# Hybrid mixer and mixture-of-experts layer: head outputs laid tile by tile, an earlier first weight load, and a new order in the expert steps

## What is computed

```python
def hybrid_mixer(h, w_in, ...):
    ...
    o = jnp.concatenate([o_a, o_b], axis=-1).astype(h.dtype)
    return o @ w_out

def hierarchical_moe(h, w_rg, b_rg, w_re, b_re, w_gate, w_up, w_down):
    g_probs = jax.nn.softmax((hf @ w_rg + b_rg).astype(jnp.float32), axis=-1)
    g_p, g_idx = lax.top_k(g_probs, 1)
    e_logits = (hf @ w_re + b_re).astype(jnp.float32).reshape(B * S, N_GROUPS, EXPERTS_PER_GROUP)
    ...
        a = jax.nn.silu(jnp.einsum('sd,edf->sef', xs, w_gate)) * jnp.einsum('sd,edf->sef', xs, w_up)
        return jnp.einsum('sef,efd->sd', a * cw[..., None], w_down)

    x = x + gt1[:, None, :] * mix
    h2 = modulate(rmsnorm(x, norm2_g[l]), sh2, sc2, dt)
    x = x + gt2[:, None, :] * ffn
```

## Time and profile before

| | before |
|---|---|
| median of 3 executions | 1078.16 us (1074.11 to 1079.16) |
| profiled execution, its own time | 1076.94 us |
| its span, first to last instruction | 1075.1 us |
| granted TensorE clock, mean | 0.974 |
| busy: TensorE, VectorE, ScalarE, GpSimd | 92%, 74%, 49%, 17% |
| moved by DMA | 206.78 MB, mean 192 GB/s |

### The profile page before, as it was taken

How to read it: one execution, slowest core, us unless ns; L and a number is a source line. 1 busy time by engine, 2 the same in 40 slices (tenths; PEclk the granted TensorE clock), 3 DMA queues, 4 the chain that set the end, 5 groups by cost and what they waited for, 6 DMA issues and landing times.

```text
span 1075.1 us, 15652 instructions
## 1 busy us (share of the span) xinstructions
PE 992.9 (92%) x5666; PEld 778.0 (72%) x5666; DVE 798.2 (74%) x1482; ACT 527.8 (49%) x921; POOL 182.1 (17%) x275
## 2 busy tenths in 40 slices
PE   3898998999999999999989999789999999999997
PEld 3668778978897998989977887356666666666642
DVE  8768669935993877959676674868888787887827
ACT  4554432654275545654561222266666656565522
POOL 0200000000100000000010000235555333433200
PEclk9799989999999999999989999899999999999999
DMA  9742533231314233230490113799999999999274
GB/s 365 228 116 81 149 97 109 80 98 50 115 54 121 77 99 99 60 99 1 156 380 16 63 40 134 273 358 350 360 365 369 366 359 364 355 352 346 111 311 169
DMA packets 79881, 206.78 MB, mean 192 GB/s; under 512 B 11750, under 2 KB 40502, under 8 KB 71628
## 3 DMA queue, kind: packets, MB, share of 16 engines
q1 hardware_dynamic: 58080, 156.25, 40.2%
q0 software_dynamic: 15120, 43.72, 12.7%
q10 hardware_dynamic: 6620, 6.00, 1.7%
HBM read 189.61 MB, written 24.71 MB: 199 GB/s over the span
## 4 chain that ended last, share of the span: by engine, by line
PE 57%; DVE 19%; DMA 13%; ACT 5%; issue 5%; SPq 0%; ACTq 0%; DVEq 0%; POOL 0%; POOLq 0%
PE PS L1957 10%; PE PS L1959 10%; PE PS L1958 10%; DMA WGU<-in_w_exp_up 9%; PE PS L2228 3%; PE PS L2022 3%; DVE AT L1425 3%; PE PS L2328 3%; PE PS L2236 2%; PE PS L2234 2%; PE PS L2235 2%; DVE ACC L1251 2%; DMA AR<-in_w_ada 2%; DVE WL L1316 1%; PE PS L2196 1%
## 5 line engine op out<-in xcount | busy, mean ns | idle before, releaser
L1957 PE MATMUL PS<-WH,HT 128*128 128x256 f32 x512 | 147.9, 289 | 5.9 <-ACT GVB L916 3.9
L1959 PE MATMUL PS<-WH,HL 128*128 128x256 f32 x512 | 145.7, 285 | 0.0
L1958 PE MATMUL PS<-WL,HT 128*128 128x256 f32 x512 | 145.7, 285 | 0.0
L1792 DVE TENSOR_TENSOR WGL<-WGU,WGH 128x1024 fp32r<-128x1024 f32 x96 | 117.0, 1220 | 22.8 <-ACT WGH L1159 21.8
L1159 ACT ACTIVATE WGH<-WGU 128x1024 fp32r<-128x1024 f32 x96 | 98.5, 1060 | 50.1 <-DMA WGU<-in_w_exp_up 40.0
L1425 DVE COPY_PREDICATED AT<-MASK,PS 128x64 f32<-128x64 uint8 x320 | 72.9, 228 | 65.3 <-PE PS L2033 46.3
L1957 PEld LDWEIGHTS PS<-WH,HT 128*128 128x128 f32 x512 | 99.3, 194 | 8.7 <-issue 8.7
L1958 PEld LDWEIGHTS PS<-WL,HT 128*128 128x128 f32 x512 | 99.3, 194 | 0.0
L1959 PEld LDWEIGHTS PS<-WH,HL 128*128 128x128 f32 x512 | 99.1, 194 | 0.0
L2234 PE MATMUL PS<-WGH,XGTH 128*96 128x512 f32 x192 | 88.4, 461 | 0.0
L1830 DVE TENSOR_TENSOR WDL<-WDN,WDH 128x2048 fp32r<-128x2048 f32 x32 | 73.3, 2292 | 16.8 <-ACT WDH L1169 16.7
(11 more groups left out here) (355 smaller groups left out, 2325.2 us busy)
## 6 DMA issues: line engine op xcount, KB each, us to landing
WGU<-in_w_exp_gate SPq DMA_DIRECT2D x32, 1024.0 KB
WGU<-in_w_exp_up SPq DMA_DIRECT2D x32, 1024.0 KB
WDN<-in_w_exp_down SPq DMA_DIRECT2D x32, 1024.0 KB, 15.6
AR<-in_w_ada POOLq DMA_DIRECT2D x32, 512.0 KB, 4.1
WF<-in_w_in SPq DMA_DIRECT2D x28, 512.0 KB, 5.5
AST<-in_w_ada SPq DMA_DIRECT2D x16, 512.0 KB, 9.0
AR<-in_w_ada_final POOLq DMA_DIRECT2D x16, 512.0 KB, 4.7
YG<-expert_rows SPq DMA_DIRECT2D x8, 1024.0 KB, 12.4
```

What stands on the lines that cost most here:

```text
L1792: V.tensor_tensor(WGL[s][:, :, ks, :], WGU[s][:, :, ks, :], WGH[(NCH * s + c) % 4][:].bitcast(F32), ALU.subtract).then_inc(wgl_ready, 1)
L1957: MM(ps, wh, xh, start=first, stop=False)
L1958: MM(ps, wh, xl, start=False, stop=False)
L1959: return MM(ps, wl, xh, start=False, stop=last)
```

## The change

1. OTH is laid [tile, head, 128] in place of [head, 1024], in the writers and in `out_product`. So the part of tiles 0 to 5 is free after their products, and the first slot is moved there: the slots are now 64, 0, 24 and 48 KB for gate and up, and 80, 16, 40 and 88 KB for down.
2. SP loads expert 0 after `wo_ready` 12 (tiles 0 to 5 done), ahead of the store of row tile 5; experts 1 to 3 follow after `wo_ready` 16 with no wait for the first gather.
3. The router-bias product is issued between heads 6 and 7 of the first three tiles; VectorE reads it before the first residual. VectorE's order is rewritten: six residuals come first, the rows of tile 4 come after `choose(0)`, and `later_column` moves behind `logits_evac(1)`.
4. New order in the expert steps on TensorE, ScalarE and VectorE.
5. Down weights are loaded as rows 2p and 2p+1 to partition p (one run of 8 KB) in place of p and p+128 (two of 4 KB); the columns of the activation follow (`j::FB`).

```diff
-        OTH = at("OTH", 64, [P, 8, T], F32R)
+        OTH = at("OTH", 64, [P, NT, 8, P], F32R)
+        GU_AT, DN_AT = [64, 0, 24, 48], [80, 16, 40, 88]
 def load_down(e, s, done):
-    sp.dma_start(WDN[s][:, :, :], w_exp_down[0, bass.ds(e, 1)].rearrange("a (j p) n -> p (a j) n", p=P)).then_inc(done, 16)
+    sp.dma_start(WDN[s][:, :, :], w_exp_down[0, bass.ds(e, 1)].rearrange("a (p j) n -> p (a j) n", p=P)).then_inc(done, 16)
 for t in range(NT - 1):
+    if t == 5:
+        sp.wait_ge(wo_ready, 12)
+        load_expert(0, 0, wexp_in[0], wdn_in[0])
     sp.wait_ge(xn_ready, t + 1)
...
-for e in range(4):
-    if e == 2:
-        sp.wait_ge(xg_in[0], 16)
+for e in range(1, 4):
     load_expert(e, e, wexp_in[e], wdn_in[e])
# ScalarE, expert_step
     if more:
+        weights_high(*after, 0, first and s < 3)
+    down_high(it, s, first)
+    if more:
         rows_high(*after, first and s < 3)
     if not (first and s == 0):
         activation_high(*((it - 1, 3) if s == 0 else (it, s - 1)))
-    if more:
-        weights_high(*after, 0, first and s < 3)
-    down_high(it, s, first)
# VectorE, after token_digits
-for half in range(2):
-    residual(0, half)
-later_column(UNITS - 1)
-for half in range(2):
-    residual(1, half)
+router_bias()
+for t in range(3):
+    for half in range(2):
+        residual(t, half)
 inverse_and_rows(0)
-for half in range(2):
-    residual(2, half)
-router_bias()
+residual(3, 0)
 inverse_and_rows(1)
-inverse_and_rows(2)
-residual(3, 0)
 residual(3, 1)
 logits_evac(0)
-inverse_and_rows(3)
+inverse_and_rows(2)
...
-inverse_and_rows(4)
+inverse_root(4)
 residual(5, 0)
 logits_evac(3)
 choose(0)
+rows_scaled(4)
+rows_shifted(4)
 residual(5, 1)
# VectorE, expert_step
     if more:
-        rows_low(*after)
+        weights_low(*after, 0)
+    v_.wait_ge(wdh_ready, 4 * it + s + 1)
+    V.tensor_tensor(WDL[s][:], WDN[s][:], WDH[s % 2][:].bitcast(F32), ALU.subtract)
     if not (first and s == 0):
         activation_low(*((it - 1, 3) if s == 0 else (it, s - 1)))
...
# TensorE, first three tiles
+if v == 6:
+    pe.wait_ge(ios, 12)
+    pe.wait_ge(shr_ready, 1)
+    ps = begin(("rb", 0))
+    MM(ps[:, 0:NG + NE], ONES[:], SHR[:], start=True, stop=True).then_inc(pj_ready, 1)
# TensorE, expert_step
+    if not (first and s < 2):
+        pe.wait_ge(att_ready, 4 * it + (s - 1))
+    gate_up_plain(it, s)
     if not (last and s == 3):
         ...
         xg_transposes((s + 1) % 2, t_ready)
     if not (first and s == 0):
         turn_activation(*before)
-    if not (first and s < 2):
-        pe.wait_ge(att_ready, 4 * it + (s - 1))
-    gate_up(it, s)
+    gate_up_split(it, s)
```

More of the change, by code:

```diff
@@ L304, in layer_kernel @@
         YB = at("YB", 96, [P, 2, D])
-        WGU = [at(f"WGU{s}", o, [P, 2, KD, FF]) for s, o in enumerate([0, 24, 48, 72])]
-        WGL = [at(f"WGL{s}", o, [P, 2, KD, FF], F32R) for s, o in enumerate([0, 24, 48, 72])]
+        GU_AT, DN_AT = [64, 0, 24, 48], [80, 16, 40, 88]
+        WGU = [at(f"WGU{s}", o, [P, 2, KD, FF]) for s, o in enumerate(GU_AT)]
+        WGL = [at(f"WGL{s}", o, [P, 2, KD, FF], F32R) for s, o in enumerate(GU_AT)]
         WGH = [at(f"WGH{c}", kb, [P, 2, KC, FF], F32R) for c, kb in enumerate([112, 116, 168, 172])]
-        WDN = [at(f"WDN{s}", o + 16, [P, FB, D]) for s, o in enumerate([0, 24, 48, 72])]
+        WDN = [at(f"WDN{s}", o, [P, FB, D]) for s, o in enumerate(DN_AT)]
         XG = at("XG", 104, [P, 2, D])
@@ L315, in layer_kernel @@
         ATTX = at("ATTX", 133, [P, FB, C])
-        WDL = [at(f"WDL{s}", o + 16, [P, FB, D], F32R) for s, o in enumerate([0, 24, 48, 72])]
+        WDL = [at(f"WDL{s}", o, [P, FB, D], F32R) for s, o in enumerate(DN_AT)]
         WDH = [at("WDH0", 184, [P, FB, D], F32R), at("WDH1", 176, [P, FB, D], F32R)]
@@ L1451, in last_head_low @@
                     v_.wait_ge(oth7_ready, g + 1)
-                    V.scalar_tensor_tensor(out=OTL[7][:, hs], in0=PJ[number[job] % 2], scalar=GN[:, 1:2],
-                                           in1=OTH[:, 7, hs].bitcast(F32), op0=ALU.mult,
+                    V.scalar_tensor_tensor(out=OTL[7][:, hs].rearrange("p (t n) -> p t n", t=4),
+                                           in0=PJ[number[job] % 2].rearrange("p (t n) -> p t n", t=4), scalar=GN[:, 1:2],
+                                           in1=OTH[:, 4 * g:4 * g + 4, 7, :].bitcast(F32), op0=ALU.mult,
                                            op1=ALU.subtract).then_inc(pj_free[number[job] % 2], 1)
@@ L1827, in expert_step @@
                 if more:
[L1828 to L1832, removed]
+                    rows_low(*after)
+                    for part in range(1, NCH):
+                        weights_low(*after, part)
                 for a in aside:
@@ L1836, in expert_step @@
                 V.tensor_tensor(ATT[:], SIL[:], GU[s % 2][0:C, FF:2 * FF], ALU.mult).then_inc(att_mul, 1)
-                if more:
-                    weights_low(*after, 2)
             extra_counts()
@@ L2134, in out_product @@
                 ts, hs = slice(t * P, (t + 1) * P), slice(half * HALF, (half + 1) * HALF)
-                return product(wo_bank(t, half), OTH[:, v, ts], OTL[v][:, ts], WOH[:, v, hs], WOL[:, v, hs], first, last)
+                return product(wo_bank(t, half), OTH[:, t, v, :], OTL[v][:, ts], WOH[:, v, hs], WOL[:, v, hs], first, last)
             pe.wait_ge(o_free, len(steps))
@@ L2161, in warm @@
                     MM(WB[0], IDENT[:], X1[:, 0, 0:HALF], start=True, stop=True)
-            for kind, i, *part in out_order:
+            for kind, i, *part in out_order[1:]:
                 if kind == "rank" and i == 1:
@@ L2174, in _ @@
                         last.then_inc(wo_ready, 1)
-                elif kind == "rb":
-                    pe.wait_ge(ios, 12)
-                    pe.wait_ge(shr_ready, 1)
-                    ps = begin(("rb", 0))
-                    MM(ps[:, 0:W], ONES[:], SHR[:], start=True, stop=True).then_inc(pj_ready, 1)
                 elif kind == "x1T":
@@ L2220, in xg_transposes, with gate_up_plain, gate_up_bank, gate_up_split @@
                 last.then_inc(done, 1)
-            def gate_up(it, s):
-                par = s % 2
-                ps = GU[par][0:C, :].rearrange("p (m f) -> p m f", m=2)
+            def gate_up_plain(it, s):
                 pe.wait_ge(wexp_in[s], 32 * it + 32)
+                pe.wait_ge(xgth_ready, 4 * it + s + 1)
+                for k in range(KS, KD):
+                    MM(gate_up_bank(s), XGTF[:, s % 2, k - KS, :], WGU[s][:, :, k, :], start=(k == KS), stop=False)
+            def gate_up_bank(s):
+                return GU[s % 2][0:C, :].rearrange("p (m f) -> p m f", m=2)
+            def gate_up_split(it, s):
+                par, ps = s % 2, gate_up_bank(s)
                 pe.wait_ge(xgt_ready, 4 * it + s + 1)
-                for k in range(KS, KD):
-                    MM(ps, XGTF[:, par, k - KS, :], WGU[s][:, :, k, :], start=(k == KS), stop=False)
                 for c in range(NCH):
@@ L2245, in extra_gate_up @@
                         for k in range(KD):
-                            last = MM(GU[0][:, col:col + C], WGU[slot][:, m, k, j * P:(j + 1) * P],
+                            last = MM(GU[0][:, col:col + C], WGU[slot][:, m, k, j::FB],
                                       XGTX[:, k, :], start=(k == 0), stop=(k == KD - 1))
@@ L2267, in turn_activation @@
                 for j in range(FB):
-                    last = TR(GU[s % 2][:, j * C:(j + 1) * C], ATT[:, j * P:(j + 1) * P], IDENT[0:C, 0:C])
+                    last = TR(GU[s % 2][:, j * C:(j + 1) * C], ATT[:, j::FB], IDENT[0:C, 0:C])
                 last.then_inc(att_turned, 1)
```

10 lines of the change are left out of this document (7 added, 3 removed).

## The result

The change makes the kernel slower: 1085.24 us median (1082.48 to 1089.01, 8 runs) against 1078.46 (1074.11 to 1083.08, 8 runs), ratio **1.0058, 95% interval 1.0032 to 1.0085**. I had forecast 1078.3 us, with a range of 1067 to 1084.6, and given slower 0.13. The profiled execution took 1086.54 us (span 1084.7), 9.6 us more than the one of before. Some of that isn't the change: the same piece of the chain (20 products of one line, 1.39 us) starts at 258.85 us where it started at 255.50, long before the output product.

The account below looks back on a forecast made before the run. The prediction took the expert weight stream to set the end, with 8.5 us of stalls. From the profiled 1076.94 us, +1.0 - 1.0 - 1.25 + 2.7 = +1.4 gave 1078.3 us, range 1067 to 1084.6.

Parts of the forecast that it names:

- Router bias earlier: Output product: the wait on BR and the slow clock behind it go, 4.8 us; less 1.6 and 0.4, a 2.8 us gain.
- the wait on LG: Transposes of tile 1: they wait for the bank until the first logits are read, 1.6 us given back.
- 0.4 us at tile 5: Output product: putting tile 4's rows behind `choose(0)` delays the one-hots by 2.5 us, costing 0.4 us at tile 5.
- Hand-over: Last store of rows to first gather: the store takes 3.3 us more behind weight loads, landing 0.5 us later than before.
- Rival C: Hand-over: the first gather takes 9.0 us, not 4.8, if weight loads still run; 1084.6 us, chance 0.11.
- First steps: Experts' first steps: plain products -1.6, GT2B -1.0, ATTL +2.75, low clock +1.2; with the hand-over's +0.5, +1.0 after step 2.
- Ten idle microseconds: Weight stream: experts 2 and 3 load without waiting for the first gather, so the slowest DMA engine starts level; -1.0 us.
- 8 KB rows: Down-weight loads: longer rows save 0.05 us per expert over 25 experts; -1.25 us, range 0 to -3.
- New order: Expert steps: nothing changes where TensorE is full; late loads must land 1.1 us into a step, not 3.9; +2.7 us once.
- B: Experts: the weight stream keeps up through 8 KB rows, all 8.5 us of stalls go; 1069.4 us, chance 0.26.
- D: Late expert steps: the new order costs nothing, as something other than ScalarE's queue bounds them; 1075.6 us, chance 0.09.

Follow-up runs that it names:

- rows4: The changed kernel with the normalised rows of tile 4 ahead of `choose(0)` again; 1083.14 us, ratio 1.0028 to the kernel before.
- bias_only: The kernel before with only part 3 (router bias earlier), the rows of tile 4 left where they were; ratio 0.9964.
- comb_nogate: comb_all without the hold of expert 3's load; ratio 0.9934 to the kernel before.
- comb_all: The changed kernel without index copies, tile 4's rows before the choice, expert 3's load held, ATT turned unstrided, GT2B awaited after step 1; 1064.88 us, ratio 0.9864.
- down8k: The kernel before with part 5 alone (down weights in 8 KB runs, columns following); ratio 0.9996.
- comb_4k: comb_all with the down weights in 4 KB runs again, the columns with them; ratio 0.9879 to the kernel before.
- static_index: The changed kernel with GpSimd's expert loop written out, without index copies and the small additions behind them; 1078.02 us, ratio 0.9984 to the kernel before.
- order_back: The changed kernel with the old expert-step order on TensorE, ScalarE and VectorE; 1079.96 us, ratio 0.9996 to the kernel before.
- pe_back: The changed kernel with only TensorE's old expert-step order; 1085.23 us, ratio 1.0057 to the kernel before.
- comb_oldorder: comb_all with the old expert-step order on TensorE, ScalarE and VectorE; ratio 0.9888 to the kernel before.

## Why the prediction was wrong

- **Router bias earlier, -2.8: measured +0.6** (up to +2.2 in the other runs). The 4.8 us are there (-6.1 at tile 0's logits), so is the wait on LG (1.40, forecast 1.6). I gave back no slow stretch behind that wait, as I had counted one behind the wait on BR. The term that failed is "0.4 us at tile 5": it was 3.7 (rows4), a wait of 1.88 on X1T at tile 4 with the lower level behind it. I had followed only the one-hots, and not that `residual(5, 1)` stands behind the moved rows, ScalarE's squares of tile 5 behind that, and its copy of X1T of tile 4 behind those. With that one placement undone the part is worth what I forecast: -3.2 at tile 7, -3.5 in all (bias_only).
- **Hand-over, +0.5 at the first gather: +5.4.** The mechanism was right, the store's price wasn't: 5.8 us more, not 3.3 (my bounds ended at 4.2). It lands when the weights queued before it do (at 692.63, the last weights at 693.5): 8.38 here, 7.75 to 8.48 in five other runs with the same loads, 2.64 with expert 3 held. Rival C had the price in the gather; that one ran free in 4.07 us. So C's place was right and its mechanism half right. That its 1084.6 lies nearest the measured time is luck: by expert 2 the loss at the hand-over is made good, and the time is lost later.
- **First steps, from +0.5 to +1.0: from +5.3 to +0.5.** The sum at expert 2 fits (+0.5), by errors that cancel. GT2B took 4.72 us, not 9.2 less 1.0, since the DMA engines lay idle (share 0.21); expert 0's plain products start 2.2 us late where the transposes before them are 5.3 late, so laying them first gave 3.1, not 1.6. TensorE's wait for ATTL there was 1.5 us, not 5.
- **Ten idle microseconds, -1.0.** Not seen by itself. Loading earlier has a price: comb_nogate against comb_all, +6.9 us.
- **8 KB rows, -1.25: -0.4 by the ratio of down8k, not to be told from nothing.** In its profile the stalls are 4.7 us less, of which 2.0 are what the longer steps take up, so 2.7 us for the stream or 0.1 per expert, inside my bounds; but that is one profile of each. What I left out is the turning of a strided ATT, **+2.0** over 29 steps. Between comb_4k and comb_all, both without the stride, the length shows no gain that can be told from nothing. Behind my figure of 0.05 stood one pair of windows and, in the last place, my own choice.
- **New order, +2.7.** Two things. "Where TensorE is full it changes nothing, the instructions are the same" is the step that failed most: it never asked what VectorE's neighbour in time does to GpSimd. It made 24 us of waits and what static_index takes back, 7 us in the medians. The other half, a late load is tolerated less, has the right sign: 5.2 us of stalls between order_back and pe_back, twice my figure, along the path I had named (WGU, WDH, ATTL). Which of ScalarE and VectorE does it stays open, and in the combined kernel it doesn't show: there the old order is not faster.
- **Rivals.** B (the stream keeps up) fell: the chain of after still stalls on WGU at 916.71 and 975.60. D (the order costs nothing) fell for this kernel with order_back and pe_back, though in the combined kernel it fits. None of the rivals had GpSimd in it, though the profile of before showed the pattern in its rows: the issue of a scatter took 2.83 us beside WDL, where more than half of them took 0.97 or less.

So the sum by measured terms, at expert 31: +0.5 at expert 2, +2.0 stride, +4.1 stalls, +6.6 us; the medians are 6.8 apart. From expert 2 on I had forecast about +0.45 (-1.0, -1.25 and +2.7), and it was +6.1: that is where the forecast was lost.

## What to carry to other kernels

When an order on one engine is rewritten, list for each moved instruction not only who waits for it but which other engine reads SBUF beside it at its new time; a small GpSimd copy in front of an indirect DMA is the first thing to look for, and the cheapest repair is to have no copy. When a layout is changed for DMA's sake, follow it to every reader: here a strided read on the full engine cost 2.0 us, and the longer rows can't be shown to have given as much. And an early load is only free if nothing small has to pass the same DMA engines before the next stage can start.

## What the runs showed of the hardware

- A GpSimd copy of 96 indices took 0.18 us in a gap of VectorE (763.51, after) or beside YB (747.51, before), 3.12 to 4.49 us up to the end of back-to-back subtractions in SBUF; the issue of a scatter took 0.97 us, or 2.83 with such a subtraction ahead of it.
- A weight load of 128 columns (96 rows) read with a stride of two float32 takes 213 ns in place of 149, its product 282 in place of 246.
- A 512 KB store issued 14 to 20 us behind 9.4 MB of loads landed about when they did (7.75 to 8.48 us), with idle engines in 2.64.
- Unexplained: from 760 to 860 us the loads of comb_all moved 31.64 MB in a share of 81.1% of the DMA engines' time, those of comb_oldorder 31.22 MB in 83.8%, the same bytes per expert in the same rows. It isn't the new order alone: after has it too and moved 29.39 MB in 79.5%, while static_index, which differs from after in the copies only, moved 31.41 MB in 81.1%. No run here tells what lets the DMA engines work with less time per byte.
